# First gate product with x's own blocks ahead of their combinations, and turned quarters and kernels placed a product later, in a one-core Griffin-style encoder layer

## The reference

```
h = x + 1/2 * SwiGLU_1(RMSNorm(x))          # D_FF = 2816
u = RMSNorm(h); [p | s | g_pool | g_ssm] = u @ w_in
z_pool = PoolMixer(p) @ w_pool_proj         # centred means over 2, 4, 8, 16 tokens
z_ssm  = GLU(gelu(BiS5(s)))                 # two-way complex diagonal state space model
h = h + (sigmoid(g_pool) * z_pool + sigmoid(g_ssm) * z_ssm) @ w_mix_out
h = h + CrossAttn(RMSNorm(h), RMSNorm(mem)) # 256 memory tokens, 4 heads
h = h + 1/2 * SwiGLU_2(RMSNorm(h))
y = RMSNorm(h)
```

## Time and profile before

| | us |
|---|---|
| median of 3 runs | 2156.42 |
| lowest, highest | 2152.35, 2160.49 |
| the profiled execution | 2166.18 |
| its span | 2164.4 |
| TensorE busy (share of the span) | 2064.8 (95%) |
| DVE, POOL, ACT busy | 1422.5, 1218.7, 637.9 |

### The profile page before, as it was taken

The page is one execution under the profiler, slowest core; times in us unless marked ns, Lnnn a source line. Parts: engine busy times, 40 slices in busy tenths (PEclk is TensorE's granted clock), DMA queues, the critical chain, the costliest instruction groups (busy, mean ns, idle before and its releaser), DMA issues.

```text
span 2164.4 us, 24480 instructions
## 1 busy us (share of the span) xinstructions
PE 2064.8 (95%) x9194; PEld 1685.0 (78%) x9194; DVE 1422.5 (66%) x1611; ACT 637.9 (29%) x979; POOL 1218.7 (56%) x802
## 2 busy tenths in 40 slices
PE   8899999999989989999998999899899999999996
PEld 4787778788878877778886888787788888887785
DVE  6677667566776979453334265546677776787778
ACT  5422322233344410001112123324232322234442
POOL 6388687778555532212332431035699998985551
PEclk9999999999999999999999999999999999999998
DMA  6423332347767462332113141111223223267763
GB/s 262 141 95 109 130 133 74 103 140 286 268 223 250 146 172 62 90 98 61 49 49 117 49 160 65 69 58 59 73 93 105 95 93 127 93 223 263 259 213 136
DMA packets 140628, 286.37 MB, mean 132 GB/s; under 512 B 12384, under 2 KB 37600, under 8 KB 140128
## 3 DMA queue, kind: packets, MB, share of 16 engines
q1 hardware_dynamic: 100496, 233.21, 31.7%
q10 hardware_dynamic: 40016, 51.61, 7.4%
HBM read 222.39 MB, written 63.42 MB: 132 GB/s over the span
## 4 chain that ended last, share of the span: by engine, by line
PE 61%; DVE 23%; DMA 6%; issue 4%; POOL 3%; ACT 1%; SPq 1%; DVEq 0%; ACTq 0%; POOLq 0%
PE ps L523 60%; DMA raw<-in_dn 4%; DVE w_lo L2341 3%; DVE xt_lo L2331 3%; DVE f_g L1778 2%; DVE h L2350 2%; DMA d_act<-f_g 1%; DVE acc L1778 1%; DVE sq L2144 1%; POOL w_lo L1106 1%; POOL start_room L1202 1%; DVE ua_lo L1778 1%; DVE sq L2327 1%; DVE sq L2182 1%; POOL raw L1185 1%
## 5 line engine op out<-in xcount | busy, mean ns | idle before, releaser
L1106 POOL TENSOR_TENSOR w_lo<-raw,w_hi 128x512 fp32r<-128x512 f32 x352 | 550.7, 1580 | 221.0 <-ACT w_hi L1341 220.7
L523 PE MATMUL ps<-xt_hi,w_hi 128*128 128x512 f32 x1320 | 517.9, 392 | 12.8 <-DVE xt_lo L2331 11.3
L523 PE MATMUL ps<-xt_lo,w_hi 128*128 128x512 f32 x1320 | 514.1, 389 | 0.0
L523 PE MATMUL ps<-xt_hi,w_lo 128*128 128x512 f32 x1320 | 514.0, 389 | 0.0
L1341 ACT ACTIVATE w_hi<-raw 128x512 fp32r<-128x512 f32 x462 | 278.6, 626 | 534.0 <-POOL raw L1134 269.9
L1114 POOL TENSOR_SCALAR w_hi<-raw 128x1024 fp32r<-128x1024 f32 x54 | 61.4, 1136 | 511.1 <-PE ps L523 504.0
L523 PEld LDWEIGHTS ps<-xt_hi,w_hi 128*128 128x128 f32 x1320 | 248.2, 188 | 75.0 <-issue 20.1
L523 PEld LDWEIGHTS ps<-xt_hi,w_lo 128*128 128x128 f32 x1320 | 248.1, 188 | 52.0
L523 PEld LDWEIGHTS ps<-xt_lo,w_hi 128*128 128x128 f32 x1320 | 248.3, 188 | 50.4
L1134 POOL TENSOR_TENSOR raw<-raw 128x512 f32<-128x512 f32 x178 | 274.6, 1552 | 12.9 <-DMA raw<-in_gu 5.6
L523 PE MATMUL ps<-ua_hi,w_hi 128*128 128x512 f32 x608 | 242.2, 398 | 10.9 <-DVE ua_lo L1778 7.0
(11 more groups left out here) (310 smaller groups left out, 2907.6 us busy)
## 6 DMA issues: line engine op xcount, KB each, us to landing
raw<-in_dn SPq DMA_DIRECT2D x264, 256.0 KB, 3.6
raw<-in_gu SPq DMA_DIRECT2D x88, 512.0 KB, 5.6
raw<-in_weights SPq DMA_DIRECT2D x54, 512.0 KB, 3.5
d_act<-acc SPq DMA_DIRECT2D x20, 512.0 KB, 2.8
d_act<-sq SPq DMA_DIRECT2D x20, 512.0 KB, 3.8
d_act<-f_g SPq DMA_DIRECT2D x20, 512.0 KB, 4.6
h<-in_x SPq DMA_DIRECT2D x16, 512.0 KB, 9.1
xt_hi<-d_act SPq DMA_DIRECT2D x8, 1024.0 KB, 7.0
```

What stands on the lines that cost most here:

```text
L523: ins = nc.tensor.matmul(out, lhsT, rhs, start=start, stop=stop)
L1106: add(lo, src, hi.bitcast(F32), op=ALU.subtract).then_inc(s_w_low["pool"], 1)
```

## The change

The first product of the first FFN now goes in `GU_ORDER`, so w11 and w12 on xb come first, then the four on xt, then s4; `GU_FIRST` stays for the second FFN (`combined_first`). POOL's xb_lo of the first pair goes to DVE. The opening's lists are put in another order to suit: the last key tile's load ahead of the key stores, x's last block ahead of the fifth tile, squares of x without interruption, sums and spreads of the norms a tile earlier, DVE's xb_lo of two pairs ahead of the values. Turned quarters move from products 4 and 6 to 5 and 7, kernels from places (10, 4), (10, 5), (14, 4), (14, 5) to (11, 0), (11, 1), (15, 0), (15, 1).

```diff
+def combined_first(f, n):
+
+    return f == 1 and n == 0
...
-TURN_AT = ((4, 0), (4, 2), (4, 4), (4, 6), (6, 0), (6, 2), (6, 4), (6, 6))
-KERN_AT = ((10, 4), (10, 5), (14, 4), (14, 5))
+TURN_AT = ((5, 0), (5, 2), (5, 4), (5, 6), (7, 0), (7, 2), (7, 4), (7, 6))
+KERN_AT = ((11, 0), (11, 1), (15, 0), (15, 1))
 TURN_OUT = tuple((n + (i + 2) // 7, (i + 2) % 7) for n, i in TURN_AT)
...
-            order = GU_ORDER if n else GU_FIRST
+            order = GU_FIRST if combined_first(f, n) else GU_ORDER
...
+                if combined_first(f, 0):
...
+                else:
+                    for kp in range(KP):
+                        wait_b_low(kp)
+                        for op in first[:2]:
+                            first_pass(op, kp)
+                    for kp in range(KP):
+                        wait_t_low(kp)
+                        for op in first[2:6]:
+                            first_pass(op, kp)
+                    for kp in range(KP):
+                        first_pass(first[6], kp)
...
+                    if k == 4 and t == 0:
+                        pe.wait_ge(s_total, 2)
+                        first_sums(1, x_sq[:, 0], L)
...
-                if k == 1:
+                if k == 0:
                     pe.wait_ge(s_const, 16 * 2)
                     pe.wait_ge(s_total, 1)
                     first_sums(0, mem_sq[:, 0], N_MEM)
-                if k == 3:
+                if k == 2:
                     pe.wait_ge(s_fac, 1)
                     first_spread(sums[:, 0, 0:N_MEM], slice(0, N_MEM)).then_inc(s_fsp, 1)
-                if k == 4:
-                    pe.wait_ge(s_total, 2)
-                    first_sums(1, x_sq[:, 0], L)
...
-            load_kv(4)
             load_x(KT - 1)
-            load_kv(5)
+            for u in range(4, 6):
+                load_kv(u)
...
                             store_values()
-                            load_kv(2 * KT - 2)
+                            for u in range(2 * KT - 2, 2 * KT):
+                                load_kv(u)
                             store_keys(0)
-                            load_kv(2 * KT - 1)
                             store_keys(1)
                             store_keys(2)
...
-                    if ops[0].key[0] == 0:
-                        pool.wait_ge(s_kvused, KT)
-                        b_low(0)
...
-            for m in range(2):
+            square_x(0)
+            root(N_MEM // P)
+            for m in range(1, KT):
                 square_x(m)
-            act.wait_ge(s_pd, 1)
+            act.wait_ge(s_pd, 2)
             nc.scalar.activation(PL["mag"], PL["dtar"], ACT.Exp)
             nc.scalar.activation(m8[:], PL["dtar"], ACT.Exp, scale=float(T))
+            nc.scalar.activation(k_mag, k_mag, ACT.Exp)
             nc.scalar.activation(PL["s"], PL["rr"], ACT.Sin)
             nc.scalar.activation(PL["c"], PL["rr"], ACT.Sin, scale=0.5).then_inc(s_pa, 1)
...
-                    splits("start")
                     act.wait_ge(s_fsp, 2)
                     act.wait_ge(s_pd, 3)
                     nc.scalar.activation(rn[:, 0:N_KEPT], start_room[:, KEPT_AT:KEPT_AT + N_KEPT], ACT.Copy).then_inc(s_kept, 1)
+                    splits(("b", 0))
                     b_high(0)
+                    splits(("b", 1))
+                    b_high(1)
                     for t in range(2):
                         values_high(t)
-                    for k in range(1, KP):
+                    splits(("b", 2))
+                    for k in range(2, KP):
                         b_high(k)
                     t_high(0)
-                    keys_high(0)
+                    for j in range(3):
+                        keys_high(j)
                     t_high(1)
-                    keys_high(1)
+                    keys_high(3)
                     act.wait_ge(s_vstore, 32)
                     t_high(2)
-                    keys_high(2)
                     act.wait_ge(s_keyst, 32 * (KT // 2 - 1))
                     t_high(3)
-                    keys_high(3)
...
+                    dve.wait_ge(s_kvused, KT)
+                    dve.wait_ge(s_kept, 1)
+                    b_low(0)
+                    b_low(1)
                     values_low(0)
                     values_low(1)
-                    dve.wait_ge(s_xb_lo_pool, 2)
                     x_sums(0, *xs(0))
-                    b_low(1)
-                    x_sums(1, *xs(1))
+                    b_low(2)
                     x_sums_low(0, *xs(0))
                     keys_low(0)
-                    b_low(2)
+                    x_sums(1, *xs(1))
+                    b_low(3)
+                    keys_low(1)
+                    x_sums_low(1, *xs(1))
+                    keys_low(2)
                     x_sums(2, *xs(2))
-                    x_sums_low(1, *xs(1))
-                    keys_low(1)
-                    b_low(3)
-                    keys_low(2)
+                    x_sums_low(2, *xs(2))
+                    keys_low(3)
                     x_sums(3, *xs(3))
-                    x_sums_low(2, *xs(2))
                     x_sums_low(3, *xs(3))
-                    keys_low(3)
```

More of the change, by code:

```diff
@@ L192, in ffn @@
                 if name[0] == "s":
-                    op.sum = sums + {"s1": 1, "s2": 2, "s3": 3, "s4": 4 if n else 5}[name]
-            sums += 4 if n else 5
+                    op.sum = sums + {"s1": 1, "s2": 2, "s3": 3, "s4": 5 if combined_first(f, n) else 4}[name]
+            sums += 5 if combined_first(f, n) else 4
             for r in raw:
@@ L392, in block_of @@
         def block_of(op):
-            _, n, _, name = op.key
-            if n:
+            f, n, _, name = op.key
+            if not combined_first(f, n):
                 return {"w11": 0, "w12": 1, "w22": 3, "s1": 2, "s2": 0, "s3": 2, "s4": 1}[name]
@@ L427, in ffn_bank @@
             return ps[(finished["pairs", f] + f + r // 2) % 4][:, r % 2]
[L429 to L432 removed]
+        gadds_before = lambda f, n: ADDS * (FT * f + n) + (ADDS_FIRST - ADDS if f and n else 0)
+        gadds = lambda f, n: gadds_before(f, n) + (ADDS_FIRST if combined_first(f, n) else ADDS)
+        gcopies_before = lambda f, n: FT * f + n + (COPIES_FIRST - 1 if f and n else 0)
         dn_evacs = lambda f, s: DN_EVACS * f + MP * DN_TARGETS[s + 1]
@@ L636, in wait_bank @@
                         n, i = before[1:]
-                        name = (GU_ORDER if n else GU_FIRST)[i]
-                        copies = ({} if n else {"s2": 1}) | {"w11": 1 if n else 2}
-                        adds = ({"w12": 2, "s2": 1, "s1": 6, "w22": 5, "s3": 3, "s4": 7} if n else
+                        other = combined_first(f, n)
+                        name = (GU_FIRST if other else GU_ORDER)[i]
+                        copies = {"s2": 1, "w11": 2} if other else {"w11": 1}
+                        adds = ({"w12": 2, "s2": 1, "s1": 6, "w22": 5, "s3": 3, "s4": 7} if not other else
                                 {"s1": 4, "s3": 1, "w22": 3, "w11": 7, "w12": 9, "s4": 8})
@@ L656, in wait_b_low, with wait_t_low @@
                 def wait_b_low(kp):
-                    if f == 0 and kp == 0:
-                        pe.wait_ge(s_xb_lo_pool, 2)
-                    else:
-                        pe.wait_ge(s_xb_lo, 2 * (kp if f == 0 else kp + 4))
+                    pe.wait_ge(s_xb_lo, 2 * (KP * f + kp + 1))
+                def wait_t_low(kp):
+                    pe.wait_ge(s_xt_lo, 2 * (KP * f + kp + 1))
                 first = [next(passes) for _ in range(7)]
@@ L1129, in product @@
                 b = [raw_block(ops[0], k) for k in range(4)]
-                first = ops[0].key[1] == 0
                 n_sum = by["s1"].sum
@@ L1141, in product @@
                 landed(ops[0], 0)
-                if first:
+                if combined_first(*ops[0].key[:2]):
                     lower("s1")
@@ L1859, in _ @@
             v.reciprocal(q["t4"], q["t4"]).then_inc(s_den, 1)
+            factor_diag(sums[:, 0], N_MEM, s_fac)
+            cp(mem_rows[:], norm[:, 2, 0:N_MEM // P])
             def add_x(m):
@@ L1863, in add_x @@
                 tt(x_sq[:, 0], x_sq[:, 0], x_sq[:, m], ALU.add, tally=totals if m == KT - 1 else step)
-            for m in range(1, 3):
+            for m in range(1, KT):
                 add_x(m)
-            factor_diag(sums[:, 0], N_MEM, s_fac)
-            cp(mem_rows[:], norm[:, 2, 0:N_MEM // P])
-            for m in range(3, KT):
-                add_x(m)
+            factor_diag(sums[:, 1], L, s_fac)
             dve.wait_ge(s_fsp, 1)
@@ L2194, in halves @@
                     add(F[0][:, C1], q["s1"], F[0][:, C1])
-                for n in range(1, FT):
+                for n in range(f, FT):
                     F = [(f_g[:, 0], f_g[:, 1]), (acc[:], sq[:])][n % 2]
```

91 lines of the change are left out of this document (33 added, 58 removed).

## The result

| | before | after |
|---|---|---|
| median of 4 executions each | 2154.39 us (2146.56 to 2160.49) | 2128.69 us (2127.82 to 2136.67) |
| ratio | | 0.9884, 95% interval 0.9858 to 0.9911 |
| profiled execution | 2166.18 us | 2128.76 us |
| its span, mean granted clock | 2164.4 us, 0.980 | 2127.0 us, 0.987 |

The kernel is faster by 1.2%, 25.7 us between the medians of this set. The forecast was 2126.9 us with a range of 2119 to 2138, so the number held. Of its three terms two held as well, and one did not: the opening gave 5.75 us instead of 8.7.

The account below looks back on a forecast made before the run. TensorE, busy 95% of the span, was taken as the bound, with time lost only in waits and low clock. 8.7 + 8.2 + 12.6 = 29.5 us, carried to the median, gave 2126.9 us, range 2119 to 2138.

Parts of the forecast that it names:

- three terms: Gains in the first FFN's gate/up stage and its opening: opening 8.7, turned quarters 8.2, kernels' matmuls 12.6 us.
- five places named: Four gate/up stretches with idle time and clock 0.74 to 0.87, plus the wait of 6.20 us before the first product.
- Part 1: Opening: the load into sq goes out earlier, so the first product begins at 71.4 instead of 80.08, 8.7 us.
- upper bound of 1.3 us: Opening, tile behind x's one-column matmuls: up to 1.3 us more if the clock holds, not counted in the sum.
- Part 2: First product, xb before xt: DVE's new list delivers operands in time, tightest margins 1.7 and 2.9 us.
- rival E: Gate/up: POOL sets the pace once TensorE no longer pauses; at 2.0 us an operation, 2189 us; 2%.
- rival B: Opening: DVE's or ACT's list over 2 us longer, TensorE waits for keys or xt_lo; gain 24, 2132.6 us; 17%.
- POOL's tables: Opening: POOL's small steps for the state space tables end at 43.4 instead of 38.73, at no cost.
- Part 3: Turned quarters moved to products 5 and 7: waits on ACT's copy shrink to 0.6 and 0.3 us, net 8.2 us.
- Part 4: Kernels' matmuls a product later: two 4.27 us waits for DVE's diagonal and the slow clock go, 12.6 us.
- Rival C: Gate/up products 5 and 7: small remaining waits keep the clock falling; gain 24 to 26, 2131.5 us; 14%.
- Rival D: Behind the changed places: a later wait meets part of the gain again; half the gain, 2141 us; 6%.

Follow-up runs that it names:

- load order run: The kernel before with only the load into sq moved ahead of the store of keys 0: 2154.22 us, ratio 1.0005 to before.
- both loads first: The changed kernel with both last key tiles' loads moved ahead of the store of the values: 2126.35 us, ratio 0.9866 to before.
- opening-only run: The changed kernel with turned quarters and kernels put back at their old places: 2148.77 us, ratio 0.9971 to before.

## Why the prediction was right, and where it wasn't

- **Where the bound is: right.** The time came out at the five places named, 26.2 us where 29.5 were forecast, and what follows moved with it. The median moved by 25.7. That parts add up was shown for the opening (the stage kept 440.4 us) and, to a microsecond or two, for quarters and kernels.
- **Part 1, the last keys' load: the mechanism right, 8.7 us mis-sized, measured 5.75.** (In the two further profiles of the changed kernel it is 7.1 and 6.7.) The step that failed is the one before it: that the load into acc "landed 8.0 us later, at 64.1". Before, TensorE came to it at 64.19 and found it there with a margin of 0.1 us. The prediction priced neither TensorE coming earlier nor the load going later, and both came true. TensorE was at 61.95, since its pause of 0.92 us ahead of x's sums was gone and the tile behind them ran at full speed (12 matmuls in 5.40 us, the upper bound of 1.3 us that the text had kept aside). The load was issued at 56.85 instead of 56.12 and landed at 65.8, 1.7 us later than before. So what was won ahead of the wait was swallowed by it, and 1.8 us of slow tile were added in this execution. Of the 5.75 us only 3.38 lie behind the start of the fourth key tile (an opening of 22.90 instead of 26.28), where the sum had all of the 8.7; the other 2.37 are that tile's earlier start (51.43 instead of 53.80), which the sum had at nothing. How much of the 2.37 is the change is open: that start lay between 50.86 and 53.43 in all profiles with the new opening, and at 53.05 with the old lists in the load order run. That the load is worth its 8.7 where the tile before it comes in time is shown by the load order run (8.6).
- **Why the load went later: a price taken from the wrong row.** Part 2 took xb_lo at 1.8 us a pair, from rows in which POOL stood idle, and the values' end at 54.2. Beside a busy POOL the two pairs took 7.46 us, the values ended at 55.5. Only DVE's earlier start (45.66 instead of the 48.1 of the text) kept it from being 2.4 us worse. The prediction named the shared port for POOL, as rival E, and left it out of DVE's list.
- **Part 2, operands in time: right in this kernel, but for another reason.** TensorE waited for neither xt_lo nor keys. The list was later than forecast (last keys at 79.25 instead of 76.5, xt_lo of the last pair at 84.46 instead of 82.1), and it was TensorE's own delay of 2.9 us that kept the margins. (With both loads first the last keys ended at 78.88, at nearly the same time, and TensorE stood there earlier.) Once the loads came in time, 1.26 us of waiting for the keys appeared: the mechanism of rival B, at the point with the margin of 1.7.
- **POOL's tables** ended at 39.8, not 43.4; costing them at nothing was right.
- **Part 3: right, 7.46 for 8.2.** The waits left at products 5 and 7 are 0.66 and 0.63 us, where 0.6 and 0.3 had been set.
- **Part 4: right, 12.96 for 12.6.** Undoing it alone costs 12.5 to 13.9.
- **Rival C, waits of 0.6 us keeping the clock down: refuted here.** The windows around both have 1.00. Two waits of 1.05 and 0.90 us close together had been enough for 0.84 before; single ones, up to 1.73 us, were not in any profile here, and two of 0.86 to 0.90 us went both ways. In the stage with the pieces of 75 matmuls, waits of 0.92 us did both as well.
  The Trainium skill (TensorE: Matmul & The Clock Gate, "A second HAM failure mode: psum-queue depth-cycling") reports a bf16 kernel in which frequent small idle gaps between groups of matmuls, cycling through PSUM banks, made the clock swing. By that rule the pieces of 75 would swing; the traces agree in some executions only (none to four of the five slow).
- **Rival D, the gain met by a later wait, and E, POOL as the pace: refuted.** The first by the opening-only run, the second by 99 us at full business with POOL at 83 (window 395 to 494 of the changed kernel).

```profile
395.00:494.00 99.00, 99.00 (x438) 82.01 (x437) 69.42 (x64) 28.09 (x46) 83.08 (x55) 1.00 0.49 173
```

The number was also helped by luck. The sum was made against a profiled execution slower than all the timed ones, with three slow pieces in it, and then carried to the median; this correction held only because the change doesn't touch that stage. And two errors partly cancel in the median: the forecast gain was 3.8 us too large (29.5 against 25.7), and the median before that it was taken from was 2.0 us higher than the one of the result's table (2156.42 against 2154.39), so that the forecast ended 1.8 us below.

## What to carry to other kernels

When you remove the last wait of a chain, look at the transfer before it: one that lands 0.1 us before it is asked for is the next wait, and what is won ahead of it is lost in it. Take the duration of an operation from a row in which the other engines do what they will be doing at the new place, above all DVE and POOL with two operands in SBUF. And where a stage's length is to be known to a microsecond, read it between two instructions of the trace; the median of one set may be several microseconds off by what happens elsewhere.

## What the runs showed of the hardware that was not expected

- A pair of xb_lo on DVE took 1.82 us with POOL idle and 3.4 to 3.9 (6.80 to 7.75 for two pairs, in all profiles with the new opening) beside POOL's 128x512 additions and subtractions, which went from 1.28 to 1.9 us. Nothing is idle in the rows of this, so no wait shows it.
- Identical pieces of 75 matmuls with identical waits of 0.92 us between them take 13.7 or 15.1 to 15.3 us, none to four of five slow in an execution. The medians of one kernel in two sets differed by 6.9 us; its two profiled executions had four slow pieces and none, and what the other executions had isn't known.
- The tile behind x's one-column sums, at the same place with the same work, took 5.40 us in some profiles and 7.09 in others; the tile behind a wait of 2.4 to 3.9 us took 3.72 to 6.74 us.
- The same pair of waits, 0.86 to 0.90 and 0.89 us at product 6's fourth quarter, was followed by a clock of 0.83 over 10 us in two profiles and of 1.00 in two others, and a single wait of 1.73 us by 1.00.
